# Prompt attention of a hybrid decoder step: the order of the row tiles within a head group

## The reference

```python
s_c = einsum('btgid,bngd->btgin', qg, kc) * scale - sl * dist_c    # compressed blocks
s_s = ... all earlier keys, for a prompt of 16 blocks of 64       # selected
s_w = einsum('btgid,bwgd->btgiw', qg, kw) * scale - sl * delta     # last 512 keys
o = gg[..., 0:1] * o_c + gg[..., 1:2] * o_s + gg[..., 2:3] * o_w
```

## Time and profile before

| | us |
|---|---|
| median of three timed runs | 2095.85 (2095.48 to 2096.1) |
| profiled execution | 2091.92 |
| its span | 2090.2 |
| prompt attention, first cast of a turned tile to the last's end | 285.8 |

### The profile page before, as it was taken

One profiled execution on the slowest core, in us unless ns is written; L12 is line 12 of the kernel. 1 busy time (PEld: TensorE's weight loads), 2 busy tenths in 40 slices (PEclk: granted clock), 3 DMA queues, 4 the chain that ended last, 5 costly groups with the idle time before them and its releaser, 6 DMA issues. The chain is left out here.

```text
span 2090.2 us, 34358 instructions
## 1 busy us (share of the span) xinstructions
PE 1936.1 (93%) x13738; PEld 1792.4 (86%) x13738; DVE 1257.1 (60%) x2239; ACT 843.5 (40%) x1693; POOL 416.8 (20%) x413
## 2 busy tenths in 40 slices
PE   6999999976898887898999999999999999999997
PEld 6999999975676663574799999999999999999997
DVE  6988864266898883512243346776666666544734
ACT  4333323354776672211242236543333333333533
POOL 2545322213655563221200002200000000000000
PEclk9999999995999997999999999999999999999999
DMA  6465531101000005443543324322222222752234
GB/s 216 123 193 167 172 133 43 42 6 41 1 1 21 1 1 208 135 154 119 187 116 87 87 76 122 111 76 82 82 73 82 72 82 73 249 182 82 84 109 139
DMA packets 212654, 210.47 MB, mean 101 GB/s; under 512 B 22775, under 2 KB 180701, under 8 KB 207184
## 3 DMA queue, kind: packets, MB, share of 16 engines
q1 hardware_dynamic: 199935, 158.20, 25.2%
q0 software_dynamic: 7104, 39.46, 5.6%
q10 hardware_dynamic: 5456, 10.62, 1.6%
HBM read 173.98 MB, written 38.43 MB: 102 GB/s over the span
## 5 line engine op out<-in xcount | busy, mean ns | idle before, releaser
L3559 PE MATMUL banks<-mixed_parts,ffn_w_h 128*128 128x264 f32 x2464 | 400.7, 284 | 0.0
L3559 PEld LDWEIGHTS banks<-mixed_parts,ffn_w_h 128*128 128x128 f32 x2464 | 341.7, 188 | 0.0
L3559 PE MATMUL banks<-mixed_parts,ffn_w_l 128*128 128x264 f32 x1232 | 252.7, 284 | 0.7 <-DVE x1T L3336 0.7
L3575 PE MATMUL banks<-mixed_parts,ffn_w_h 128*128 128x264 f32 x1232 | 199.5, 284 | 0.0
L3559 PEld LDWEIGHTS banks<-mixed_parts,ffn_w_l 128*128 128x128 f32 x1232 | 192.6, 188 | 0.9 <-issue 0.9
L3575 PEld LDWEIGHTS banks<-mixed_parts,ffn_w_h 128*128 128x128 f32 x1232 | 170.1, 188 | 0.0
L89 PE MATMUL banks<-fm_hT_h,fm_w_l 128*128 128x352 f32 x648 | 146.8, 335 | 1.4 <-DVE hT_l L918 1.4
L89 PE MATMUL banks<-hT_l,fm_w_h 128*128 128x352 f32 x648 | 140.0, 324 | 0.0
L89 PE MATMUL banks<-fm_hT_h,fm_w_h 128*128 128x352 f32 x648 | 139.8, 323 | 0.0
L680 POOL TENSOR_TENSOR fm_w_l<-fm_raw,fm_w_h 128x512 fp32r<-128x512 f32 x54 | 95.2, 1763 | 216.2 <-ACT fm_w_h L754 216.0
L1845 PE MATMUL banks<-ident,scores 128*128 128x128 f32 (+1 forms) x592 | 96.8, 289 | 35.8 <-DVE probsT_l L1991 22.6
(11 more groups left out here) (541 smaller groups left out, 4332.2 us busy)
## 6 DMA issues: line engine op xcount, KB each, us to landing
ffn_raw<-in_w_ffn_in_dram SPq DMA_DIRECT2D x44, 512.0 KB, 5.1
act_copy<-ffn_act_rows SPq DMA_DIRECT2D x44, 264.0 KB, 2.2
mixed<-act_copy SPq DMA_DIRECT2D x44, 264.0 KB, 5.7
fm_raw<-in_w_in_dram SPq DMA_DIRECT2D x44, 256.0 KB, 3.0
ffn_down_raw<-in_w_ffn_out_dram SPq DMA_DIRECT2D x10, 1024.0 KB, 5.1
early_w_raw<-in_w_in_dram SPq DMA_DIRECT2D x32, 256.0 KB, 3.0
merge_raw<-in_w_in_dram SPq DMA_DIRECT2D x32, 256.0 KB, 2.9
merge_raw<-in_w_o_dram SPq DMA_DIRECT2D x32, 256.0 KB, 3.0
```

The lines of the kernel that those rows point to most:

```text
L3559: mm = pe.matmul(ps[:, bank + h, 0:HC], w[:, kt, :], m.mix_r[m.cell(h, kt)][:, m.MIX[name], part, :], start=(fresh and kt == 0 and j == 0) ...
L3575: mm = pe.matmul(ps[:, 2 * j + c, 0:HC], w[g % NSLOT][:, j, :], x[:, c, :], start=(kt == 0 and n3 == 0), stop=(kt == FT - 1 and n3 == 2))
```

## The change

Batches of a head group are put in another order. Before, group 0 goes through the row tiles 0 to 7 and group 1 from 7 down to 0. After, group 0 goes 0, 4, 1, 5, 2, 6, 3, 7 and group 1 the same list backwards. Nothing else is edited: `steps_at`, `factors_at`, the buffers and the engine programs go by the list as before. What changes with it is which batch's tiles and which batch's scores are interleaved.

```diff
-    batches = [(0, qt) for qt in range(QT)] + [(1, qt) for qt in reversed(range(QT))]
+
+    order = [i // 2 + QT // 2 * (i % 2) for i in range(QT)]
+    batches = [(0, qt) for qt in order] + [(1, qt) for qt in reversed(order)]
     NBAT = len(batches)
```

## The result

The kernel with the new order takes 2108.49 us (median of five; 2105.63 to 2112.1) beside 2096.1 for the kernel before in the same comparison: ratio 1.0047, 95% interval 1.0029 to 1.0064. The forecast was 2094.4 with a range to 2102; the change makes the kernel slower, by about 0.5%.

The account below looks back on a forecast made before the run. VectorE (DVE) was taken to bound the 285.8 us prompt-attention stage, with only 44.55 us idle movable. Terms -0.8, -0.8, +2.0, -0.2, -1.4 and -0.2 sum to -1.4 us: 2095.85 becomes 2094.4 us, range 2088 to 2102.

Parts of the forecast that it names:

- the clock rival: Slower: waits ending six short stretches drop TensorE's clock in the long row tiles behind; +7.6 us, 2103.4; chance 0.17.
- the sum: Prompt-attention stage: changes in DVE idle over the stretches, grouped by tiles turned, add to -1.4 us.
- The slower rival: Low TensorE clock behind six short stretches, 1.5 us each: +9, with the forecast's -1.4 giving 2103.4 us; chance 0.17.
- n=5, 12, 13 and 14: Stretches turning that many key tiles: -1.4 us for 5, +0.5 per stretch for 12, -0.8 for 13, -0.8 for 14.
- n=11: Stretches turning 11 key tiles, 4>1 and 4>0: TensorE near its limit beside short scores, +0.5 us each.
- n=7 and 9: Stretches turning 7 or 9 key tiles: idle of 7 from 5.5 to 5.3 us, that of 9 stays 4.9.
- DVE busy: VectorE's work in the stage, 241.25 us, stays within 2 us of 241.
- POOL: GpSimd adds no term; with tables built in the last-but-one stretch, the last scaling is late by 2.6 us at most.
- the fixed wait: Each stretch: DVE waits 1.19 us while ACT runs two exponents before the next cast; unchanged, term 0.
- Faster by the early stretches: Rival: denser 0>4 raises the clock and 4>1 keeps it; 4.6 us go, -6.0 in all, 2089.8 us; chance 0.20.
- Balance: Rival: long turns complement long scores, all fourteen changed stretches idle 2.15 us; -7.8 us, 2088; chance 0.08.

Follow-up runs that it names:

- eight products in group 0: Old order with eight unread TensorE products behind row tiles 1, 2 and 3 of group 0 only, against the kernel before: 2096.64 us, 0.9986.
- the ten products: New order plus ten unread TensorE products before the first turn after row tiles 0 to 3: 2096.94 us, 0.9989 of the kernel before; in old order 2101.67 us, 1.0013.

## Why the prediction was wrong

**The step that failed** is the weight given to the clock rival: the sum has no term for the clock behind the short row tiles, and against the rival stood only "after the 2.38 us wait the clock was 1.00 throughout the next stretch". That was one wait in one trace. First, it isn't a fixed property of that place: with eight products in group 0, the same wait in the unedited group 1 was followed by 1.2 GHz, and 1>0 was at 0.77. In the kernel before, too, waits of 2.01 and 2.04 us (ends of 1>2 and 2>3) stood ahead of stretches at 0.90 and 0.91. Second, the wait of the new order is longer. I took it from a row of the old one, behind 2>1, where the next scores have 128 columns. With 640 to 896 columns it is 3.3 to 4.4 us at five of the seven short ends: in 2>6 it consists of the next row tile's exponents, a cast, the subtraction and the scaling. The parts were readable: the exponents and the cast of the earlier trace rows, 1.75 us from 657.64 to DVE's subtraction, and two scalings, seen above as 1.82 for 896 columns. At 3>7 and 3>6 it is 2.31 and 2.65 though the scores are as long; with nine tiles, `steps_at` leaves three behind the last score step, with five only one, so PE probably has more to do there. The clock fell at these two as well. My walk through 1>5 priced the stretch and not what PE does at its end. What the runs showed in place of the missing term: about 48 us at 1.2 GHz for 22.5, and 12.6 us of the stage, which the ten products gave back.

**The slower rival is what happened.** Its place and its reason (no slack on PE in the long row tiles) are shown by the ten products; that nearly half of the low clock lies in the short ones, where it costs little, it didn't say. Its price of 1.5 a spell is right in the mean: taken out, spells gave back idle of 2.1 us (5>2), 2.0 (6>2), 1.8 (4>0), 1.2 (6>3) and 1.2 (5>1). Its 2103.4 was 5 us short of the median. It had a chance of 0.17. The sign set for it, 0.8 or less in four of 5>2, 6>3, 6>2 and 5>1, did not come (0.87, 0.92, 0.89, 0.94), nor did the forecast's 1.00: a mean clock of about 0.9 over a long stretch was enough to cost a microsecond or two. The stage, 296.1 us, left the 280 to 292 that the prediction named.

What I cited of the Trainium skill, "TensorE: Matmul & The Clock Gate", section "HAM oscillation — how this bites in real kernels", is a fall to the low clock in each round that ends in a PE wait; its example waits for a transfer. The trace agrees with it in that all seven stretches behind short ends are below 1.00 (0.87 to 0.95, from 4>1 to 4>0), with DMA at 0.00 or 0.01 in them, though in three places the clock fell before the last wait or just as it began.

**The sum came near at nearly the full clock, in part by luck.** It said that the stage's DVE idle goes from 44.55 to 43.15. With ten products it was 283.5 - 240.59 = 42.9. But the 44.55 contain spells of the old order, and the ten products took 2.4 us of idle out of 1>2, 2>3 and 3>4 there. At like clocks the order's own part is then an estimated +0.8 (42.9 against 44.55 - 2.4 = 42.1) and not -1.4. Nor does each term hold: n=5, 12, 13 and 14 were 0.3 to 0.7 too low in their pairs (n=12: 5.2 for 4.7), n=11 2.0 too low, with a spell still in 4>1, and n=7 and 9 about 1.1 and 1.2 too high (n=9: 3.7 for 4.9). At the clocks it really had, the long ones idled 3.8 to 4.6 instead of 2.1 to 2.6.

**DVE busy, POOL, the fixed wait** were as said: 242.62 for 241.25; POOL's tables hardly made the last scaling late (in the last stretch PE waits 0.42 us for POOL, 0.16 before); and the wait for the cast is there, 0.93 in the lines of 2>6. **Faster by the early stretches**: not alone, since 0>4 ends in the longest wait, but with the clock held the old order's 2>3 and 3>4 gave 2.7 us. **Balance** didn't come: with ten products the fourteen changed stretches idle 2.7 on average, not 2.15 (and the seven that this was taken from have 2.09 by the earlier trace rows).

## What to carry to other kernels

The sums of busy time were nearly unchanged, and with the clock held the mix cost little: 283.5 us, against an estimated 283.1 for the old order (285.8 less the 2.7 that ten products gave in three stretches). A schedule with work in turns of unequal size can still cost 0.5% by leaving TensorE idle at the turn. So with each new order, work out how long TensorE waits in and at the end of the short turns, from the parts of these waits, and look whether what stands behind has TensorE near its limit. One place that kept the clock in one trace is no evidence that another will. Products that nobody reads are a cheap test of such a theory, as long as they are shorter than the wait.

## What was not expected of the hardware

Waits of 2.31 and 2.65 us in the new order (3>7, 3>6) were followed by 0.95 and 0.89, a wait of 2.38 in the old one by 1.00, and the same wait by 1.2 GHz in another run: the length of one wait doesn't tell it alone. The programs' times also vary more than the 0.2% that I named: runs of the kernel before lay between 2091.9 and 2107.8 us. Their granted clock goes with it: of 88 such runs beside the experiments, the 27 under 2096 us have a mean clock of 0.966 to 0.969 over the whole program, the 8 over 2104 us one of 0.960 to 0.962. Where in the program their spells lie is not on record. Two profiles of the new order have stages of 296.1 and 296.0 us, but unedited stretches of the old order differ by the clock (1>0: 11.2 us at 1.00, 12.6 at 0.77). The first cast stood at 510.1 to 521.3; 2.0 us of this are the longer score steps of 0>4, and the rest lies in front of the stage, where all of them are the same program. What moves it there was not tried.
